# Gated expert rows turned by VectorE, and only filled result rows written, by GpSimd

## The chip, the cores and the metric

The kernel runs on one core of one Trainium2 chip. The metric is device time in microseconds (us). TensorE (PE) multiplies matrices into eight PSUM banks, VectorE (DVE) and ScalarE (ACT) read the banks, GpSimd (POOL) and SyncE (SP) mostly start DMA transfers.
## The reference

Two transformer blocks over 1024 tokens of width 1024. The first mixes tokens with gated linear attention and stick-breaking attention. The second has sliding-window attention, an mLSTM, cross attention and a mixture of 32 experts. Only that last part is touched:

```
expert_idx, gates = two experts for each token, with their weights
for each expert e, xb = the rows of its tokens:
    hb = silu(xb @ w_g[e]) * (xb @ w_u[e])      # 1024 -> 512 hidden columns
    yb = hb @ w_d[e]                            # 512 -> 1024
out[token] += yb[row] * gate                    # two rows for each token
```

1024 tokens with two experts each make 2048 assignments, 64 per expert on average. All matrices are float32.

## The kernel before, in words

Each expert has a block of `CAP` = 96 rows in three groups of `TG` = 32. An expert with more tokens gets spare blocks of 32 rows at the end; rows without a token are empty. For one block, TensorE (function `expert` of the tensor program) does this in order:

1. `group_products` (L1622): for each of three groups, 64 products of 32 rows of the turned block `XT` with the gate and up weights, spread over the four 32-partition quadrants (`QUADS`) of the group's bank.
2. `turn_hidden(0)` (L1628): when the hidden rows of groups 0 and 1 are there, two 128x128 products with the identity turn them into a bank; ACT's `hidden_home` copies them to `HIDT`.
3. `turn_block` (L1613): turns the gathered rows `XG` of the next block; VectorE (`block_ready`, L3148) scales them into `XT`.
4. `turn_hidden(1)` for group 2, and ACT's copy.
5. `down_products` (L1638): 96 products with the down weights into two banks. They wait for the hidden rows and for the result of the block before to be out of these banks (`y0_out`, `y1_out`).

ACT's `silu_of` turns a group's gate part into `SILU`; VectorE's `hidden_of` (L3154) multiplies it with the up part into `HID`. ACT copies the first result bank to `YO` (L1742, a helper's line that many operations have), VectorE the second (L3204). Both first wait for `y_stored`, the store of the block two before, which had the same `YO`. ACT then issues four stores (`store_block`, L2221), one for each quadrant, 32 partitions x 3 groups x 1 KB each: all 96 rows, empty or not, go to `y_of_slot` in DRAM.

GpSimd's loop (L3531): when block k is turned it copies the indices of block k+2 (L3535) and gathers its rows from `xn` with an indirect DMA of 96 descriptors of 4 KB (`gather_block`, L3519). A row without a token has an index beyond the bound and is skipped. SyncE loads each expert's three weight matrices (2 MB each, L3652) into one of two sets of buffers: gate and up when the group products of the expert two before are over, down when its down products are.

At the end GpSimd gathers two result rows for each token (L3555), which are added with their gates and normed. Much earlier (L3440) GpSimd fills the spare blocks of `y_of_slot` with zeros out of the buffer of `masks`, which ACT later overwrites with a gate tile.

## Time and profile before

| What | Value |
|---|---|
| median of three runs | 2068.24 us (2066.67 to 2074.23) |
| profiled execution, span | 2067.1 us |
| PE busy | 1994.4 us, 96% |
| DVE, ACT, POOL busy | 932.4, 583.1, 376.2 us |
| DMA moved | 360.51 MB |

The span of the profiled execution lies within the runs' spread; its median lies 1.1 us above, and no separate time of that execution is given beyond its span. The experts stand in the last quarter, 1463.84 to 2016.15 us: in the slices of 52 us the DMA engines are 90% busy or more there, while before they are mostly under 30%. "Idle before" is time in which an engine stood still ahead of an instruction, with what ended it. "To landing" is the time from the issue of a transfer to its completion.

### The profile page before, as it was taken

The numbers are of one execution on the slowest core, as the hardware profiler recorded it, in microseconds if no ns is written. First come the engines' busy times: TensorE is split into PE (matmuls) and PEld (weight loads), VectorE is DVE, ScalarE is ACT, GpSimd is POOL, SyncE is SP. The second block draws the span as 40 slices with busy tenths as digits, with TensorE's granted clock in tenths as the row PEclk, the third lists the DMA queues.
The fourth block names the chain that finished last, engine by engine and source line by source line (L and its number), as shares of the span: only waits on it lengthen the run. The fifth ranks groups of instructions, "written<-read, shape, count | busy, mean of one in ns | idle before, by whom it ended". The sixth has DMA issues, their size and how long they took to land.

```text
span 2067.1 us, 37980 instructions
## 1 busy us (share of the span) xinstructions
PE 1994.4 (96%) x15588; PEld 1136.0 (55%) x15588; DVE 932.4 (45%) x1543; ACT 583.1 (28%) x1076; POOL 376.2 (18%) x317
## 2 busy tenths in 40 slices
PE   8999999999899999999999999998999999999997
PEld 6476564765434445454446454565666666666563
DVE  3434553455676753586666674344511111111115
ACT  4123231433575220243123422242111111111113
POOL 0304333325252003004000233000100000000003
PEclk9999999999999999999999999999999999999999
DMA  9221220212525023600030412012899999999987
GB/s 396 84 82 36 81 95 28 94 31 87 173 102 173 31 103 64 166 1 1 0 122 11 143 42 64 1 41 91 346 398 402 406 407 414 416 405 412 404 355 269
DMA packets 104554, 360.51 MB, mean 174 GB/s; under 512 B 20536, under 2 KB 59856, under 8 KB 90128
## 3 DMA queue, kind: packets, MB, share of 16 engines
q1 hardware_dynamic: 58016, 280.37, 34.7%
q0 software_dynamic: 16368, 55.85, 8.0%
q10 hardware_dynamic: 30080, 23.09, 3.4%
q8 instruction: 58, 0.95, 0.2%
q14 instruction: 32, 0.26, 0.0%
HBM read 319.16 MB, written 45.49 MB: 176 GB/s over the span
## 4 chain that ended last, share of the span: by engine, by line
PE 72%; DMA 13%; DVE 8%; ACT 4%; issue 2%; ACTq 1%; POOL 0%; DVEq 0%; POOLq 0%; SPq 0%; PEldq 0%
PE bank L741 18%; DMA y_of_slot<-HT 13%; PE bank L734 12%; PE bank L951 9%; PE bank L1622 8%; PE bank L1638 4%; ACT work L1742 3%; PE bank L977 2%; PE bank L1037 2%; DVE O L2291 1%; DVE work L2291 1%; PE bank L809 1%; PE bank L1375 1%; PE bank L1152 1%; PE bank L849 1%
## 5 line engine op out<-in xcount | busy, mean ns | idle before, releaser
L1742 ACT ACTIVATE HT<-bank 64x256 f32<-64x256 f32 (+2 forms) x215 | 91.9, 432 | 452.5 <-PE bank L1622 197.0
L1742 ACT ACTIVATE work<-bank 128x512 f32<-128x512 f32 (+5 forms) x246 | 123.2, 520 | 327.4 <-PE bank L741 96.0
L1742 ACT ACTIVATE work<-work 128x1024 f32<-128x1024 f32 (+5 forms) x200 | 158.9, 806 | 170.4 <-DVEq L149 114.7
L734 PE MATMUL bank<-slots,HT 128*128 128x512 f32 (+2 forms) x576 | 184.1, 475 | 2.0 <-ACT HT L1742 1.5
L1622 PE MATMUL bank<-slots,HT 128*32 128x256 f32 x3136 | 172.4, 379 | 2.5 <-DVE HT L3148 1.6
L1622 PE MATMUL bank<-work,HT 128*32 128x256 f32 x3072 | 168.9, 379 | 0.4 <-issue 0.4
L3268 POOL TENSOR_TENSOR work<-work 128x1024 f32<-128x1024 f32 (+1 forms) x64 | 112.0, 1750 | 241.8 <-DVEq L149 160.6
L3154 DVE TENSOR_TENSOR HT<-HT,bank 64x256 f32<-64x256 f32 x97 | 41.1, 423 | 242.8 <-ACT HT L1742 242.4
L1622 PEld LDWEIGHTS bank<-slots,HT 128*32 128x32 f32 x3136 | 103.1, 110 | 68.8 <-issue 3.2
L734 PEld LDWEIGHTS bank<-slots,HT 128*128 128x128 f32 x576 | 98.3, 190 | 76.6 <-issue 71.2
L1622 PEld LDWEIGHTS bank<-work,HT 128*32 128x32 f32 x3072 | 102.4, 110 | 64.2 <-issue 1.0
L741 PE MATMUL bank<-HT,slots 128*128 128x512 f32 x256 | 116.4, 606 | 3.7 <-ACTq L149 2.5
L951 PE MATMUL bank<-slots,HT 128*128 128x512 f32 x256 | 114.8, 595 | 0.6 <-issue 0.6
L3204 DVE COPY HT<-bank 128x256 f32<-128x256 f32 x32 | 13.6, 425 | 204.9 <-DMA y_of_slot<-HT 139.0
L3535 POOL COPY index<-token_list 128x1 uint32 x32 | 5.9, 184 | 465.9 <-PE bank L1613 465.9
L1638 PE MATMUL bank<-slots,HT 128*32 128x256 f32 x1568 | 88.1, 380 | 0.7 <-ACT HT L1742 0.6
L1638 PE MATMUL bank<-work,HT 128*32 128x256 f32 x1536 | 86.2, 380 | 0.0
L951 PE MATMUL bank<-HT,slots 128*128 128x512 f32 x192 | 85.7, 594 | 0.5 <-ACT gate_row L1742 0.5
L741 PEld LDWEIGHTS bank<-HT,slots 128*128 128x128 f32 x256 | 49.2, 194 | 64.3 <-issue 62.9
L2447 DVE COPY_PREDICATED work<-masks,bank 128x512 f32<-128x512 uint32 x56 | 49.9, 891 | 71.4 <-PE bank L977 71.1
L1742 ACT ACTIVATE work<-O 128x1024 f32<-128x1024 f32 (+1 forms) x51 | 50.5, 990 | 95.7 <-DVEq L149 87.4
L951 PEld LDWEIGHTS bank<-slots,HT 128*128 128x128 f32 x256 | 46.6, 190 | 50.1 <-issue 50.0
(352 smaller groups left out, 3091.1 us busy)
## 6 DMA issues: line engine op xcount, KB each, us to landing
slots<-in_w_e_gate_dram SPq DMA_DIRECT2D x17, 2048.0 KB, 13.5
slots<-in_w_e_up_dram SPq DMA_DIRECT2D x17, 2048.0 KB
slots<-in_w_e_down_dram SPq DMA_DIRECT2D x17, 2048.0 KB, 17.4
work<-in_w_e_gate_dram SPq DMA_DIRECT2D x16, 2048.0 KB, 13.2
work<-in_w_e_up_dram SPq DMA_DIRECT2D x16, 2048.0 KB
work<-in_w_e_down_dram SPq DMA_DIRECT2D x16, 2048.0 KB
slots<-in_w_in_dram SPq DMA_DIRECT2D x8, 2048.0 KB, 8.7
slots<-in_w_ada_dram SPq DMA_DIRECT2D x6, 2048.0 KB, 15.3
```

The lines of the kernel that those rows point to most:

```text
L734: ins = pe.matmul(bank, lhsT, rhs, start=(n == 0), stop=(n == len(pairs) - 1))
L741: ins = pe.matmul(bank, of, x[:, k, :], start=(first and k == 0), stop=(last and k == 3), skip_group_check=True)
L951: ins = pe.matmul(bank, *pairs, start=(k == 0), stop=(k == NK - 1))
L977: ins = pe.matmul(bank[:, (j - j0) * P:(j - j0 + 1) * P], k[:, j * P:(j + 1) * P], q[:, j * P:(j + 1) * P], start=True, stop=True)
L1037: ins = pe.matmul(bank[:, 0:256], x[:, k], w[:, k], start=(first and k == 0), stop=(last and k == 3), skip_group_check=True)
L1622: ins = pe.matmul(GROUP_BANKS[g][QUADS[q], 0:QW], XT[:, k, g * TG:(g + 1) * TG], w[:, k, (q % 2) * QW:(q % 2 + 1) * QW], start=(k == 0), s ...
L1638: ins = pe.matmul(DOWN_BANKS[g // 2][QUADS[q], (g % 2) * QW:(g % 2 + 1) * QW], HIDT[:, g // 2, f % 2, at:at + TG], wd[:, f, q * QW:(q + 1) ...
L1742: return act.activation(o, i, f, bias=bias, scale=scale, **more)
L2291: line(dve.tensor_tensor(o, a, b, op))
L2447: empty(lambda b: dve.copy_predicated(s, bcast(m.unsqueeze(1), [P, NT, P // n, n // 2]), b.rearrange("p (j a h) -> p j a h", j=NT, h=n // 2)))
L3154: dve.tensor_tensor(HID[at:at + 64, g // 2, :], SILU[64:P, g, :], GROUP_BANKS[g][64:P, 0:QW], ALU.mult)\
L3268: line(pool.tensor_tensor(o, a, b, op))
```

## The change: what it does

Two things change in the experts' part.

First, TensorE no longer turns the hidden rows. VectorE writes a group's hidden rows to partitions 64 to 127 of `HID`, waits for its own write, and turns them with two 32x32-block transposes of 64x128 elements into `HIDT`. Such a transpose turns each block in place of its own, so the hidden features come out in another order, and the rows of the down weights are permuted on the host in the same order (`turned_hidden_rows`). ACT's two copies go too.

Second, the result is written by GpSimd with three indirect DMAs per block, one for each group: 128 partitions x 1 KB, each piece with its own destination index out of `piece_list`, which VectorE makes once. The index of a piece whose row is empty is beyond the bound, and the piece is skipped. In GpSimd's loop these writes stand behind the wait for `y0_out` and `y1_out` of the block, and the gather of the next turn of the loop behind them. The zero fill now covers all of `y_of_slot`: 154 blocks of 32 rows instead of 58.

```diff
 
 
+def turned_hidden_rows():
+
+    f, c, h, j = np.meshgrid(*(np.arange(n) for n in (DE // P, 2, 2, TG)), indexing="ij")
+    return (DE // 2 * h + P * c + TG * f + j).reshape(-1)
...
+    put("slot_of_piece", r % TG + TG * np.arange(TGS)[None, :])
+    put("piece_of_y", (r % TG + TG * np.arange(EXPERTS * TGS)[None, :]) * (D // QW) + r // TG)
...
-        HID = cut(HT_flat[:, 6 * D:6 * D + 2 * QW], 2)
-        HIDT = HT_flat[:, 7 * D:7 * D + 4 * P].rearrange("p (a c n) -> p a c n", a=2, c=2)
-        GROUP_BANKS, TURN_BANKS, HIDDEN_BANKS = banks[0:TGS], banks[4:6], (banks[3], banks[0])
+        HID = cut(HT_flat[:, 6 * D:6 * D + TGS * QW], TGS)
+        HIDT = cut(HT_flat[:, 7 * D:7 * D + TGS * P], TGS)
+        GROUP_BANKS, TURN_BANKS = banks[0:TGS], banks[4:6]
...
-        y_experts = y_dram[0:EXPERTS * CAP].rearrange("(b p) d -> b p d", p=CAP)
+        y_pieces = y_dram.rearrange("r (q c) -> (r q) c", c=QW)
...
-            def turn_hidden(a, turned):
-                for c in range(2):
-                    ins = pe.transpose(HIDDEN_BANKS[a][:, c * P:(c + 1) * P], HID[:, a, c * P:(c + 1) * P],
-                                       const("ident"))
-                ins.then_inc(turned, 1)
-
             def down_products(wd, groups, full):
 
                 for g in groups:
                     for f in range(DE // P):
-                        at = 64 * (g % 2) + TG * (f // 2)
                         for q in range(4):
                             ins = pe.matmul(DOWN_BANKS[g // 2][QUADS[q], (g % 2) * QW:(g % 2 + 1) * QW],
-                                            HIDT[:, g // 2, f % 2, at:at + TG], wd[:, f, q * QW:(q + 1) * QW],
+                                            HIDT[:, g, f * TG:(f + 1) * TG], wd[:, f, q * QW:(q + 1) * QW],
                                             start=(f == 0), stop=(f == DE // P - 1))
...
                     list_products()
-                pe.wait_ge(hidden_ready, it * 6 + 3 * x + 2)
-                turn_hidden(0, hidden_turned)
                 pe.wait_ge(rows_gathered[1 - x], it * 16 + 16 * (x + 1))
                 turn_block(1 - x, tokens_turned)
-                pe.wait_ge(hidden_ready, it * 6 + 3 * x + 3)
-                turn_hidden(1, hidden_turned)
                 pe.wait_ge(weights_in[x][2], it * 16 + 16)
 
                 pe.wait_ge(y0_out, it * 2 + x + 1)
                 pe.wait_ge(y1_out, it * 2 + x + 1)
-                pe.wait_ge(hidden_back, it * 4 + 2 * x + 1)
+                pe.wait_ge(hidden_ready, it * 6 + 3 * x + 2)
                 down_products(wd, (0, 1), down_full)
-                pe.wait_ge(hidden_back, it * 4 + 2 * x + 2)
+                pe.wait_ge(hidden_ready, it * 6 + 3 * x + 3)
                 down_products(wd, (2,), down_full)
 
             for x in range(2):
...
-            def hidden_home(a, back):
-                func(HIDT[:, a, :, :], cut(HIDDEN_BANKS[a], 4)[:, 0:2, :], ACT.Copy).then_inc(back, 1)
-
-            def store_block(block, y, sem):
-                rows = y_experts[bass.ds(block, 1)].rearrange("a (g r) (q c) -> q r (a g) c", r=TG, c=QW)
-                for q in range(4):
-                    act.dma_start(rows[q], cut(y[QUADS[q], :], TGS)).then_inc(sem, 16)
...
+            def expert(it, x, first=False):
+
+                for g in range(TGS):
+                    act.wait_ge(group_full, it * 6 + 3 * x + g + 1)
+                    silu_of(g, silu_ready)
+                if not first:
+                    act.wait_ge(y_stored[x], it * 48)
+                act.wait_ge(down_full, it * 4 + 2 * x + 1)
+                func(YO[x][:, 0:HALF], DOWN_BANKS[0], ACT.Copy).then_inc(y0_out, 1)
...
-                    for g in range(TGS):
-                        act.wait_ge(group_full, it * 6 + 3 * x + g + 1)
-                        silu_of(g, silu_ready)
-                    for a in range(2):
-                        act.wait_ge(hidden_turned, it * 4 + 2 * x + a + 1)
-                        hidden_home(a, hidden_back)
-                    act.wait_ge(y_stored[x], it * 64 + 64)
-                    act.wait_ge(down_full, it * 4 + 2 * x + 1)
-                    func(YO[x][:, 0:HALF], DOWN_BANKS[0], ACT.Copy).then_inc(y0_out, 1)
-                    act.wait_ge(y0_out, it * 2 + x + 2)
-                    act.wait_ge(y1_out, it * 2 + x + 2)
-                    store_block(it * 2 + x, YO[x], y_stored[x])
-            act.wait_ge(y_stored[0], 64 * (EXPERTS // 2 + 1))
+                    expert(it, x)
+            act.wait_ge(y_stored[0], 24 * EXPERTS)
...
+            ts(ASSIGNED, SPN, (CAP + 1 - TG) / TG - BELOW, float(TG), ALU.add, ALU.mult)
...
-            def hidden_of(g, ready):
-                at = 64 * (g % 2)
-                dve.tensor_tensor(HID[at:at + 64, g // 2, :], SILU[64:P, g, :], GROUP_BANKS[g][64:P, 0:QW], ALU.mult)\
-                    .then_inc(ready, 1)
+            def hidden_of(g, made, count, ready):
+
+                dve.tensor_tensor(HID[64:P, g, :], SILU[64:P, g, :], GROUP_BANKS[g][64:P, 0:QW], ALU.mult).then_inc(made, 1)
+                dve.wait_ge(made, count)
+                for c in range(2):
+                    ins = dve.transpose(HIDT[64 * c:64 * c + 64, g, :], HID[64:P, g, c * P:(c + 1) * P])
+                ins.then_inc(ready, 1)
...
-                for x in range(2):
-                    dve.sem_inc(y_stored[x], 64)
...
+                each = [P, EXPERTS, TGS]
+                tt(cut(PIECES, EXPERTS), bcast(const("slot_of_piece").unsqueeze(1), each), bcast(ASSIGNED.unsqueeze(2), each),
+                   ALU.is_ge)
+                stt(piece_list[:, :], PIECES, BEYOND_Y, const("piece_of_y"), ALU.mult, ALU.add)
...
-                dve.wait_ge(y_stored[x], it * 64 + 64)
+                if not (first or second):
+                    dve.wait_ge(y_stored[x], it * 48)
...
-            line(dve.memset(HID[64:P, 1, :], 0.0))
...
-            pool.dma_start(y_spares.rearrange("b p d -> p b d"),
-                           zeros[0:TG, :].unsqueeze(1).to_broadcast([TG, SPARE, D])).then_inc(spare_cleared, 16)
+            pool.dma_start(y_dram.rearrange("(b p) d -> p b d", p=TG),
+                           zeros[0:TG, :].unsqueeze(1).to_broadcast([TG, SPARE + EXPERTS * TGS, D])).then_inc(spare_cleared, 16)
...
                     pool.wait_ge(index_ready, it * 2 + x + 1)
                     pool.sem_inc(pool_passed, 1)
                     gather_block(x, XG[x], rows_gathered[x])
+                    pool.wait_ge(y0_out, it * 2 + x + 2)
+                    pool.wait_ge(y1_out, it * 2 + x + 2)
+                    pool.tensor_copy(pieces[x][:, :], piece_list[:, bass.ds((it * 2 + x) * TGS, TGS)]).then_inc(pieces_ready, 1)
+                    pool.wait_ge(pieces_ready, it * 2 + x + 1)
+                    pool.sem_inc(pool_passed, 1)
+                    for g in range(TGS):
+                        pool.indirect_dma_start(y_pieces, bass.IndirectOffsetOnAxis(ap=pieces[x][:, g:g + 1], axis=0),
+                                                YO[x][:, g * QW:(g + 1) * QW], None, bounds_check=EXPERTS * CAP * 4 - 1,
+                                                oob_is_err=False).then_inc(y_stored[x], 16)
...
-    for name in ("w_e_gate_2", "w_e_up_2", "w_e_down_2"):
+    for name in ("w_e_gate_2", "w_e_up_2"):
         arrays[f"in_{name}_dram"] = by_partition(_np.asarray(inputs[name])[0])
+    arrays["in_w_e_down_2_dram"] = by_partition(_np.asarray(inputs["w_e_down_2"])[0][:, turned_hidden_rows(), :])
```

On TensorE, one expert inside the loop stood so before (L1622 group products, L1628 turns of hidden rows, L1613 turn of the next block, L1638 down products):

```order
L1622 MATMUL bank<-slots,HT 32x256 [waits tokens_ready]
L1622 MATMUL bank<-slots,HT 32x256 x95
L1628 MATMUL bank<-cst,HT 128x128 [waits hidden_ready]
L1628 MATMUL bank<-cst,HT 128x128
L1613 MATMUL bank<-cst,HT 128x96 [waits rows_gathered1]
L1613 MATMUL bank<-cst,HT 128x96 x7
L1628 MATMUL bank<-cst,HT 128x128 [waits hidden_ready]
L1628 MATMUL bank<-cst,HT 128x128
L1638 MATMUL bank<-slots,HT 32x256 [waits hidden_back]
L1638 MATMUL bank<-slots,HT 32x256 x31
```

and stands so now (L1635, L1626 and L1644 are the same three steps):

```order
L1635 MATMUL bank<-slots,HT 32x256 [waits tokens_ready]
L1635 MATMUL bank<-slots,HT 32x256 x95
L1626 MATMUL bank<-cst,HT 128x96 [waits rows_gathered1]
L1626 MATMUL bank<-cst,HT 128x96 x7
L1644 MATMUL bank<-slots,HT 32x256 [waits hidden_ready]
L1644 MATMUL bank<-slots,HT 32x256 x31
```

The four turns of hidden rows are gone, and the turn of the next block, which waits for its gathered rows, is all that stands between the two kinds of product.

GpSimd's loop, both of its blocks, before:

```order
L3535 ISA [waits tokens_turned]
L3535 COPY index<-token_list 128x1
L3519 DMA HT<-xn,index 96x1024 [waits index_ready]
L3535 ISA [waits tokens_turned]
L3535 COPY index<-token_list 128x1
L3519 DMA HT<-xn,index 96x1024 [waits index_ready]
```

and the first of them now, up to the next block's first wait:

```order
L3533 ISA [waits tokens_turned]
L3533 COPY index<-token_list 128x1
L3517 DMA HT<-xn,index 96x1024 [waits index_ready]
L3539 ISA [waits y1_out,y0_out]
L3539 COPY pieces<-piece_list 128x3
L3543 DMA y_of_slot<-HT,pieces 19712x256 [waits pieces_ready]
L3543 DMA y_of_slot<-HT,pieces 19712x256 x2
L3533 ISA [waits tokens_turned]
```

The second gather of the loop now comes behind a wait for the block's result and behind three writes in the same queue.

## Rows read from the trace of the kernel before

**Rows 1.** The page: span and busy times.

```profile
span 2067.1 us, 37980 instructions
PE 1994.4 (96%) x15588; PEld 1136.0 (55%) x15588; DVE 932.4 (45%) x1543; ACT 583.1 (28%) x1076; POOL 376.2 (18%) x317
```

**Rows 2.** Chain that ended last, in order (start us, us, what): two experts; a store.

```profile
1638.37 10.36 PE bank L1622 x192
...
1655.44 10.36 PE bank L1622 x192
1665.80 0.37 PE bank L1628 x2
1666.17 0.66 PE bank L1613 x8
1666.83 0.36 PE bank L1628 x2
...
1710.22 31.73 DMA y_of_slot<-HT
```

**Rows 3.** Instructions in order of time: before the experts, experts 0, 14 to 15, 28, the spare.

```profile
1447.13 1.22 PE L1597 MATMUL bank<-work,cst 128*128 128x256 f32 x2 [4.08 <-DVEq L149]
...
1463.84 10.57 PE L1622 MATMUL bank<-slots,HT 128*32 128x256 f32 x192 [1.58 <-DVE HT L3148]
...
1717.29 0.33 SPq L3652 DMA_DIRECT2D slots<-in_w_e_gate_dram  x1
...
1719.25 0.98 POOL L3519 DMA_INDIRECT HT<-xn,index  x1 [0.86 <-POOL index L3535]
1723.52 10.54 PE L1622 MATMUL bank<-work,HT 128*32 128x256 f32 x192
...
1958.24 0.44 PE L1628 MATMUL bank<-cst,HT 128*128 128x128 f32 x2 [1.87 <-DVE HT L3154]
...
2021.65 0.44 PE L1628 MATMUL bank<-cst,HT 128*128 128x128 f32 x2 [0.95 <-DVE HT L3154]
```

**Rows 4.** Waits, 1500 to 2067 us (us in total, times, longest us).

```profile
ACT HT L1742 <- DMA y_of_slot<-HT: 154.5, 20, 11.6
```

**Rows 5.** Stretches (length, PE PEld DVE ACT POOL busy, PEclk, DMA share, GB/s).

```profile
1600.00:1700.00 100.00, 100.00 (x1773) 60.55 (x1766) 14.86 (x33) 17.68 (x37) 6.59 (x11) 1.00 1.01 407
1448.00:1450.00 2.00, 2.00 (x6) 1.50 (x6) 1.59 (x5) 1.28 (x1) 0.00 (x0) 0.50 0.99 426
```

**Rows 6.** DMA queues, 1600 to 1700 us: packets, MB, share of 16 engines.

```profile
q1 hardware_dynamic: 2534, 36.95, 90.3%
q10 hardware_dynamic: 2533, 2.23, 6.6%
q0 software_dynamic: 672, 1.50, 4.5%
```

**Rows 7.** DMA issues (count, KB, us to landing): 1500 to 1600; 1900 to 2000.

```profile
slots<-in_w_e_gate_dram SPq DMA_DIRECT2D x3, 2048.0 KB, 15.2
...
work<-in_w_e_gate_dram SPq DMA_DIRECT2D x3, 2048.0 KB, 11.6
```

**Rows 8.** The tile xn, 1480 to 2067 us: its gathers.

```profile
DMA to landing us min/median/max: 2.7/10.4/14.8
```

**Rows 9.** Groups of instructions by form, VectorE, 1455 to 1520 us.

```profile
L3154 DVE TENSOR_TENSOR HT<-HT,bank 64x256 f32<-64x256 f32 x9 | 3.8, 423 | 20.4 <-ACT HT L1742 20.3
L2291 DVE TENSOR_TENSOR work<-work 128x32 f32<-128x32 f32 x2 | 0.4, 193 | 0.1
```

**Rows 10.** The zero fill: its issue, its landing, what stands behind it.

```profile
808.94 1.04 POOL L3440 DMA_DIRECT2D y_of_slot<-masks  x1 [0.30 <-POOL masks L3439]
...
DMA to landing us min/median/max: 41.0/41.0/41.0
...
953.83 1.28 POOL L3268 TENSOR_TENSOR work<-slots 128x512 f32<-128x512 f32 x1 [143.85 <-DVEq L2304]
...
1078.63 1.23 ACT L1742 ACTIVATE masks<-bank 128x512 f32<-128x512 f32 x2 [0.18 <-ACT work L1742]
```

More of the change, by code:

```diff
@@ L634, in program @@
         spare_map = ctx.enter_context(nc.sbuf_tensor("spare_map", [P, SPARE + 1], I32))
+        piece_list = ctx.enter_context(nc.sbuf_tensor("piece_list", [P, EXPERTS * TGS], U32))
+        pieces = [ctx.enter_context(nc.sbuf_tensor(f"pieces{x}", [P, TGS], U32)) for x in range(2)]
+        pieces_ready = sem("pieces_ready")
         index = [ctx.enter_context(nc.sbuf_tensor(f"index{x}", [P, 1], U32)) for x in range(3)]
@@ L662, in program @@
         y_stored = [sem(f"y_stored{x}") for x in range(2)]
-        (tokens_turned, tokens_ready, group_full, silu_ready, hidden_ready, hidden_turned, hidden_back, down_full,
+        (tokens_turned, tokens_ready, group_full, silu_ready, hidden_made, hidden_ready, down_full,
          y0_out, y1_out, index_ready) = (sem(n) for n in (
-             "tokens_turned", "tokens_ready", "group_full", "silu_ready", "hidden_ready", "hidden_turned", "hidden_back",
+             "tokens_turned", "tokens_ready", "group_full", "silu_ready", "hidden_made", "hidden_ready",
              "down_full", "y0_out", "y1_out", "index_ready"))
-        (sp_rows, sp_weights, sp_down_weights, sp_turned, sp_ready, sp_group, sp_silu, sp_hidden, sp_hidden_turned,
-         sp_hidden_back, sp_down, sp_y, sp_stored, sp_index, sp_passed) = (sem("spare_" + n) for n in (
-             "rows", "weights", "down_weights", "turned", "ready", "group_full", "silu", "hidden", "hidden_turned",
-             "hidden_back", "down", "y", "stored", "index", "passed"))
+        (sp_rows, sp_weights, sp_down_weights, sp_turned, sp_ready, sp_group, sp_silu, sp_hidden_made, sp_hidden,
+         sp_down, sp_y, sp_stored, sp_index, sp_passed) = (sem("spare_" + n) for n in (
+             "rows", "weights", "down_weights", "turned", "ready", "group_full", "silu", "hidden_made", "hidden",
+             "down", "y", "stored", "index", "passed"))
         pool_passed, spare_cleared = sem("pool_passed"), sem("spare_cleared")
@@ L2251, in _ @@
                     act.wait_ge(sp_stored, s * 64 + 64)
[L2252 removed]
+            act.wait_ge(y_stored[1], 24 * EXPERTS)
             act.sem_inc(moe_over, 1)
@@ L3053, in _ @@
             BELOW = 0.5 / TG - 0.5
+            BEYOND_Y = 2.0 ** 20
             line(dve.memset(OF_EXPERT, 1.0))
@@ L3185, in gates_and_slots, with expert @@
                 copy(slot_id[:, :], SLOT)
+                each = [P, EXPERTS, TGS]
+                tt(cut(PIECES, EXPERTS), bcast(const("slot_of_piece").unsqueeze(1), each), bcast(ASSIGNED.unsqueeze(2), each),
+                   ALU.is_ge)
+                stt(piece_list[:, :], PIECES, BEYOND_Y, const("piece_of_y"), ALU.mult, ALU.add)
                 dve.sem_inc(routed, 1)
-            def expert(it, x, first=False):
+            def expert(it, x, first=False, second=False):
                 for g in range(TGS):
@@ L3206, in _ @@
             line(dve.memset(token_list[:, :], 0))
-            line(dve.memset(HID[64:P, 1, :], 0.0))
             dve.wait_ge(tokens_turned, 1)
             block_ready(tokens_ready)
-            for x in range(2):
-                expert(0, x, first=(x == 0))
+            expert(0, 0, first=True)
+            expert(0, 1, second=True)
             with dve.Fori(1, EXPERTS // 2) as it:
```

19 lines of the change are left out of this document (9 added, 10 removed).

## The prediction

> **What bounds the kernel now.** I read the page first, then the chain, the waits, the stretches, the DMA queues and the landings. TensorE is busy 96% of a span of 2067.1 us [rows 1]. The experts run from 1463.84 to 2016 us, about 552 us [rows 3]. In the chain one expert is four steps of TensorE ahead of the down products, 10.36 + 0.37 + 0.66 + 0.36 us [rows 2]. The group products of one expert and the next start at 1638.37 and 1655.44 us [rows 2], so a period is 17.07 us, and the down products are the remaining 5.32. TensorE has no idle time from 1600 to 1700 us [rows 5]. So TensorE bounds this part, but in the same stretch the DMA share is 1.01 [rows 5]: the DMA engines never rest either. Two bounds lie side by side, and an edit on TensorE alone can be worth no more than the distance to the other.
>
> That distance needs two numbers. The first is the lead of the weights. Gate weights are issued at 1717.29 us [rows 3] and are needed two experts on, when the group products behind those of 1723.52 start: 1740.6, that is 23.3 us later. The gate matrix lands after 15.2 us early in the experts and 11.6 late [rows 7]; the up matrix follows it, 2.1 MB at 407 GB/s [rows 5] = 5.2 us. So both are there 2.9 us ahead of need early and 6.5 late. The lead grows by 3.6 us in some 23 experts, 0.16 us each: the DMA engines' pace is 17.07 - 0.16 = 16.9 us per expert.
>
> The second is how the queues share the engines. In 100 us q1 (weights) passed 2534 packets and q10 (stores) 2533 [rows 6], though one weight packet has 16 KB and one store packet 1 KB. Per expert that is 3 x 128 + 48 = 432 and 4 x 96 + 64 = 448 asked for. Equal counts mean that a queue with work gets one packet in turn, whatever its size. The stores therefore crawl: one takes 31.73 us [rows 2], ACT waits 154.5 us for them [rows 4], and at times this reaches TensorE (1.87 us at 1958.24 [rows 3]).
>
> **The change, part by part.** *TensorE's turns.* 0.37 + 0.36 = 0.73 us per expert, 32 experts: 23.4 us less work on the engine that bounds [rows 2]. All of it is on the path now.
>
> *VectorE's transposes.* Two of 64x128 per group. The trace shows none. From below, an operation of 32 columns takes 193 ns; from above, one of 256 columns 423 ns [rows 9]. I take 0.25 us, 0.5 for two; at worst 0.85. The hidden rows of group 2 are ready about 0.4 (ACT) + 0.42 + 0.1 + 0.5 = 1.4 us after the group products, at worst 1.8. TensorE asks for them after the turn (0.66) and two thirds of the down products (3.5), at 4.2 us. So 0 on the path; the cover is 2.4 us or more. Group 1 is ready sooner still. VectorE is 15% busy there [rows 5]. In the spare block nothing covers them: TensorE's turn took 0.44 us [rows 3], and ACT's copy behind it is as long, 0.9 to 1.0 with the handover, against 0.6: -0.4. The memset dropped (64x256) and the small operation added before the first expert: -0.1.
>
> *Fewer bytes.* 2048 of 3072 rows are filled, so of q10's 6.6% a third goes: 0.066 x 17.07 / 3 = 0.37 us per expert. The skipped pieces still pass as descriptors, as skipped rows of the gather do: q0 has 672 packets for six gathers, 112 each = 96 + 16, all rows counted, but only 1.50 MB [rows 6]. I give these 0.1 us. DMA pace: 16.9 - 0.37 + 0.1 = 16.6 us per expert, against TensorE's 16.34. So the DMA engines become the bound.
>
> *The queue.* q0 now gets 3 x (128 + 16) + 112 = 544 packets per expert, 34 per engine. The weights queue has 27 per engine. At one in turn, q0 keeps up only if the weights queue stands empty for part of each expert. A turn is 17.07 / 27 = 0.63 us, so writes and gather need 34 x 0.63 = 21.5 us, and 2 to 3 more for issue and completion (the fastest gather took 2.7 [rows 8]). In the loop GpSimd issues the gather of block k+3 behind the writes of block k, about 7 us after the down products of k; TensorE wants it at its turn in k+2, 16.34 + 10.4 = 26.7 us after them. It has 20 us where it now has 32 (it is issued at 1719.25, inside the down products [rows 3]). So TensorE stops at rows_gathered from the first experts on, in stops of one to four us, until the weights' lead is so long that q1 runs empty. What this costs is lead: DMA work is the same, but TensorE can't use up the lead of the weights.
>
> *The sum.* The weights of the last expert come 30 x (16.9 - 16.6) = 9 us sooner. If TensorE ends with the same lead over need as before (6.5 us), the experts end 9 + 0.7 (the last expert is shorter) = 9.7 us sooner. The lead at which q1 runs empty is longer: gate weights with nothing ahead need 2 + 2 x 5.2 = 12.4 us, a lead of 22.6 - 12.4 = 10 us. That takes back up to 3.7: 6.0 us. If the lead could be used up, 9.7 + 6.5 = 16.2. I take 7.5 us, between 9.7 and 6.0, and 0.5 for the edges: 8 us. The profiled span of 2067.1 becomes 2059; the median lies 1.1 higher: 2060 us.
>
> *Zero fill.* 154 blocks for 58: 41.0 x 154 / 58 = 109 us, ending near 918. Two loads of 2 MB go beside it; GpSimd reads them first at 953.83, 35 us behind the end of the whole fill; ACT writes over the zeros' source at 1078.63 [rows 10]. Moving 4.2 MB takes some 10 us at 407 GB/s. Cost 0, with 25 us of cover even if the loads waited for the whole fill; past that each us would count.
>
> *ACT.* Two copies and four issues per expert go; ACT is 18% busy there [rows 5], worth 0. GpSimd gains three indirect issues of 0.98 us [rows 3] per expert and is 7% busy [rows 5]: 0 by itself.
>
> **A rule that speaks against this.** The trace shows one packet per turn between q1 and q10 [rows 6]; for q0 it has only gathers of seven packets per engine, 10.4 us to land [rows 8], which is about seven turns and the fixed part. The Trainium skill, "DMA: Bandwidth & Descriptors", section "Queues, rings and completion order", says that a DMA engine drains a whole packet of some 9 to 17 descriptors from one ring before it goes to the next. By that rule q0 would not starve. What q0 would then give is the first rival; the rows on q1 and q10 do not agree with the rule.
>
> **Rivals.** *First: q0 keeps up, the weights are used just in time.* For it: GpSimd's queue has other descriptors than the two that were counted, and no row shows it backlogged. Against: the length of the gathers. Lead used up: 16.2 + 0.5, and some stops: 2068 - 16 = 2052 us.
>
> *Second: the full gain.* TensorE stays the bound: 23.4 us, and some 3 us of stops like that of 1.87 us [rows 3]: 2041 us. For it: the DMA share may count waiting, and the pace be elastic. Against: the landings moved only 0.16 us per expert while TensorE took 17.07.
>
> *Third, slower: q0's turns cost what they do now, and the stops cost clock.* If a turn stays 0.63 us and the seven more that q0 needs add 0.06 us each, an expert takes 27 x 0.63 + 0.4 = 17.4 us, 0.35 more than now: +11 us. Besides, after TensorE stood idle for 4.08 us before 1447.13 us [rows 3] its granted clock was 0.50 from 1448 to 1450 [rows 5], the lower of its two levels (1.2 GHz for 2.4). Three spells of some 3 us at half pace are +5. Less the half us of edges: 2084 us with the clock, 2079 without. It decides from a turn of 0.62 us on, which is 0.01 below today's; against it stand the third fewer real pieces.
>
> *Fourth: the pieces are not skipped or the fill delays the mLSTM part:* no gain, 2068 or a little over.
>
> **Chances.** Forecast 0.54, first rival 0.21, full gain 0.05, third 0.13, fourth 0.07. A run of this kernel tells about 0.5%, 10 us, from no change. The forecast's own range is 2050 to 2069; a third of its chance is beyond 10 us faster (0.18), the rest within (0.35). First rival: 0.18 faster, 0.03 within. Full gain 0.05 faster. Third: 0.09 slower, 0.04 within. Fourth: 0.05 within, 0.02 slower. Rounded: faster 0.41, within 0.5% 0.48, slower 0.11. The range, 2046 to 2077, leaves the full gain and the worst of the third outside.
>
> **What would show it.** L1628 and ACT's copies gone, transposes of 0.2 to 0.3 us; q0 at about 544 packets per expert and q10 at none; TensorE idle ahead of the turn of the next block (L1626 now) behind the transfer of xn, 1 to 4 us in about every third expert; gathers landing in 15 to 25 us; gate weights in 7 to 11 us, not 12 to 15; a mean period of 16.8 us. The forecast is wrong if TensorE waits for weights (first rival), if it never waits (second), or if PEclk falls under 1 between 1480 and 2000 us (third).

## The result: slower by 0.9%, by stops of TensorE beside GpSimd's issues

The changed kernel took 2087.91 us in its first measurement (median of 4, 2086.47 to 2089.8) against 2067.45 for the kernel before (2065.7 to 2074.23): ratio 1.0091 [1.0076, 1.0106], some 19 us slower. The forecast was 2060, with 2077 as its upper end. The page of the profiled execution:

```profile
span 2086.7 us, 37598 instructions
PE 2009.3 (96%) x15458; PEld 1168.4 (56%) x15458; DVE 991.8 (48%) x1739; ACT 539.4 (26%) x996; POOL 478.1 (23%) x445
```

TensorE has 130 instructions fewer than in [rows 1] and is busy 15 us longer. The chain that ended last shows where, in the columns of [rows 2]:

```profile
1709.43 0.81 PE bank L1626 x8
1710.24 5.32 PE bank L1644 x96
1715.56 5.28 PE bank L1635 x92
1720.84 0.10 issue
1720.94 0.68 PE bank L1635 x6
1721.62 0.09 issue
1721.70 5.42 PE bank L1635 x94
1727.13 0.81 PE bank L1626 x8
1727.94 5.32 PE bank L1644 x96
1733.26 5.23 PE bank L1635 x93
```

The turns are gone: one step of 0.81 us stands for 0.37 + 0.66 + 0.36, and the down products still take 5.32. But the group products (L1635) go from 1715.56 to 1727.13, 11.57 us for 10.36 in [rows 2], and are broken in the middle. The period is 1733.26 - 1715.56 = 17.70 us, not 17.07. So 0.58 us are won and 1.2 lost, 0.6 us per expert. Over the whole part it is less, because TensorE stands still in a few experts of the kernel before too (periods of 17.9, 17.6 and 19.0 us), and its mean period is 17.18 us: by the two traces the experts take 15.4 us longer (1465.66 to 2033.35 against 1463.84 to 2016.09 us), they begin 1.8 us later, and what stands behind them, the spare block first, takes 2.3 us more, 19.6 us in all. The same expert by engine, in order of time, with the idle time before each in brackets (these views count a step from the start of its first product, the chain from the end of the product before it, so the group products are 10.54 us here where the chain has 10.36, and 11.75 where it has 11.57):

```profile
1715.16 4.66 PEld L1635 LDWEIGHTS bank<-slots,HT 128*32 128x32 f32 x87
1716.29 0.18 POOL L3539 COPY pieces<-piece_list 128x3 uint32 x1 [10.91 <-DVE HT L3203]
1717.35 1.02 POOL L3543 DMA_INDIRECT y_of_slot<-HT,pieces  x1 [0.88 <-POOL pieces L3539]
1718.67 0.99 POOL L3543 DMA_INDIRECT y_of_slot<-HT,pieces  x1 [0.30 <-issue]
1719.97 0.98 POOL L3543 DMA_INDIRECT y_of_slot<-HT,pieces  x1 [0.30 <-issue]
1720.19 0.16 PEld L1635 LDWEIGHTS bank<-slots,HT 128*32 128x32 f32 x6 [0.37 <-issue]
1720.95 0.19 PEld L1635 LDWEIGHTS bank<-slots,HT 128*32 128x32 f32 x6 [0.59 <-issue]
1720.98 0.38 ACT L1742 ACTIVATE HT<-bank 64x256 f32<-64x256 f32 x1 [6.48 <-remote]
1721.72 1.47 PEld L1635 LDWEIGHTS bank<-slots,HT 128*32 128x32 f32 x30 [0.59 <-issue]
```

GpSimd issues the three writes from 1717.35 to 1720.95. TensorE's weight loads run on for 2.47 us, stop at 1719.82, and go on in spurts of six with 0.37, 0.59 and 0.59 us between them. Nothing that the program waits for ended these gaps ("issue"): no wait stands within the group products. ACT's silu of group 0 starts 5.6 us after the start of the group products (1715.38), where it is 3.7 us in the kernel before when ACT has no store to wait for:

```profile
1655.26 10.54 PE L1622 MATMUL bank<-work,HT 128*32 128x256 f32 x192
1658.96 0.38 ACT L1742 ACTIVATE HT<-bank 64x256 f32<-64x256 f32 x1 [3.83 <-PE bank L1622]
```

The stops are in every expert from the second on, the first that has a GpSimd write beside it; the first expert, with none beside it, took 10.57 us.

The DMA engines are not what stops it. The queues in 1600 to 1700 us (as [rows 6]), that stretch (as [rows 5]), and the landings of the gathers (as [rows 8]):

```profile
q1 hardware_dynamic: 2512, 36.47, 90.9%
q0 software_dynamic: 1485, 3.11, 9.5%
...
1600.00:1700.00 100.00, 98.97 (x1690) 64.33 (x1686) 26.36 (x69) 9.94 (x23) 22.38 (x32) 1.00 1.00 396
...
DMA to landing us min/median/max: 2.1/7.1/12.8
```

PEclk is 1.00, the gathers come sooner than before, and from 1500 us to the end of the experts TensorE waits neither for weights nor for xn.

### The profile page after: what moved, and what is told of

It reads as the page before. It is cut to its first block, busy times and chain, and to the rows that moved or that the text cites. A ratio compares the mean times of both kernels' runs of the same rounds, so it can differ in the third digit from the quotient of the medians.

```text
span 2086.7 us, 37598 instructions
## 1 busy us (share of the span) xinstructions
PE 2009.3 (96%) x15458; PEld 1168.4 (56%) x15458; DVE 991.8 (48%) x1739; ACT 539.4 (26%) x996; POOL 478.1 (23%) x445
## 4 chain that ended last, share of the span: by engine, by line
PE 85%; DVE 7%; ACT 3%; issue 2%; DMA 1%; POOL 0%; DVEq 0%; ACTq 0%; POOLq 0%; SPq 0%; PEldq 0%
PE bank L754 18%; PE bank L1635 17%; PE bank L747 12%; PE bank L964 9%; PE bank L1644 8%; PE bank L1050 2%; PE bank L990 2%; ACT work L1742 2%; PE bank L1165 1%; DVE work L2282 1%; DVE O L2282 1%; PE bank L1626 1%; PE bank L822 1%; PE bank L1388 1%; DMA slots<-in_w_ada_dram 1%
## 5 line engine op out<-in xcount | busy, mean ns | idle before, releaser
L1742 ACT ACTIVATE HT<-bank 64x256 f32<-64x256 f32 (+1 forms) x150 | 67.8, 452 | 558.5 <-PE bank L1635 213.2
L1635 PE MATMUL bank<-slots,HT 128*32 128x256 f32 x3136 | 187.6, 380 | 5.3 <-DVE HT L3141 1.4
L1635 PE MATMUL bank<-work,HT 128*32 128x256 f32 x3072 | 184.4, 380 | 3.1
L1635 PEld LDWEIGHTS bank<-slots,HT 128*32 128x32 f32 x3136 | 125.2, 110 | 64.7 <-issue 26.2
L1635 PEld LDWEIGHTS bank<-work,HT 128*32 128x32 f32 x3072 | 124.5, 110 | 60.0 <-issue 23.5
L3543 POOL DMA_INDIRECT y_of_slot<-HT,pieces x96 | 95.7, 996 | 48.1 <-POOL pieces L3539 26.4
L1644 PE MATMUL bank<-slots,HT 128*32 128x256 f32 x1568 | 89.4, 384 | 3.4 <-DVE HT L3150 2.7
L1644 PE MATMUL bank<-work,HT 128*32 128x256 f32 x1536 | 86.2, 380 | 0.0
L3539 POOL COPY pieces<-piece_list 128x3 uint32 x32 | 5.8, 182 | 338.6 <-DVE HT L3203 338.6
## 6 DMA issues: line engine op xcount, KB each, us to landing
y_of_slot<-masks POOLq DMA_DIRECT2D x1, 19712.0 KB, 105.7
```

The lines of the kernel that those rows point to most:

```text
L1635: ins = pe.matmul(GROUP_BANKS[g][QUADS[q], 0:QW], XT[:, k, g * TG:(g + 1) * TG], w[:, k, (q % 2) * QW:(q % 2 + 1) * QW], start=(k == 0), s ...
L1644: ins = pe.matmul(DOWN_BANKS[g // 2][QUADS[q], (g % 2) * QW:(g % 2 + 1) * QW], HIDT[:, g, f * TG:(f + 1) * TG], wd[:, f, q * QW:(q + 1) * QW],
L1742: return act.activation(o, i, f, bias=bias, scale=scale, **more)
L3543: pool.indirect_dma_start(y_pieces, bass.IndirectOffsetOnAxis(ap=pieces[x][:, g:g + 1], axis=0), YO[x][:, g * QW:(g + 1) * QW], None, boun ...
```

## The experiments

Three theories at first: A, GpSimd's issues hold TensorE up; B, the traffic of the pieces does; C, VectorE's transposes do. Each group below ran on one chip with the kernel before beside it. The code shown is shortened. A "job" is a set of runs taken together on one chip. A period is the mean from the turn of block 3 to that of block 31: 17.18 us in the kernel before, 17.66 in the changed one.

### Which part of the change: four runs in one job

**Turns alone.** After's `hidden_of` and down weights, before's `store_block` and zero fill:

```diff
-                    for g in range(TGS):
-                        pool.indirect_dma_start(y_pieces, ...).then_inc(y_stored[x], 16)
+                    store_block(it * 2 + x, YO[x], y_stored[x])     # ACT
```

> VectorE turns the hidden rows (with the permuted down weights), but ACT stores the blocks as before and only the spare blocks are filled with zeros. Theory A (GpSimd's three indirect writes per expert hold up TensorE and its signals while they are issued): no such writes, so the group products take 10.36 us again, ACT's silu of group 0 starts 3.5 us after their start, and the 0.73 us per expert of TensorE's turns are gained as far as the weights allow: 2045 to 2060 us. Theory B (the traffic of the written and skipped pieces disturbs the DMA engines or TensorE): the same. Theory C (VectorE's transposes disturb TensorE or the signals): the stalls in the group products stay, 11.6 us for them, 2080 us or more.

**Writes alone.** Before with after's piece list, zero fill and GpSimd writes; TensorE turns the hidden rows:

```diff
-                    store_block(it * 2 + x, YO[x], y_stored[x])     # ACT
+                    for g in range(TGS):
+                        pool.indirect_dma_start(y_pieces, ...).then_inc(y_stored[x], 16)
```

> TensorE turns the hidden rows as in the kernel before, and only the stores are changed: GpSimd writes the pieces with three indirect transfers per expert, and all of the result is filled with zeros. Theories A and B: the group products take 11.6 to 11.7 us instead of 10.36 in all experts but the first, with silu of group 0 some 2.1 us late, so the whole is the kernel before plus 31 x 1.25 = 39 us: 2100 to 2110 us, slower than the changed kernel by the turns' 0.73 us x 32. Theory C: no stalls, 2060 to 2070 us.

**All pieces skipped.**

```diff
+                ts(PIECES, PIECES, 0.0, None, ALU.mult)
+                ts(PIECES, PIECES, 1.0, None, ALU.add)
                 stt(piece_list[:, :], PIECES, BEYOND_Y, const("piece_of_y"), ALU.mult, ALU.add)
```

> The changed kernel with every piece's index beyond the bound: the same three indirect transfers per expert, but no piece is written (the experts' results don't reach memory, only the spare blocks' do). Theory A (the issue itself): the stalls stay as they are, group products 11.6 us, 2086 to 2089 us. Theory B (the pieces' traffic): the stalls shrink or go, 2045 to 2065 us. Theory C: stalls stay.

**Two writes later.**

```diff
                     for g in range(TGS):
+                        if g == 1 and not last:
+                            pool.wait_ge(group_full, it * 6 + 3 * x + 4)
                         pool.indirect_dma_start(...)
```

> The changed kernel, but GpSimd issues only the first write at once and the other two when the first group of the next block is over, that is between two signals of TensorE's (the first issue ends 3.0 us after the start of the group products, the signal is due at 3.5, the other two run from some 4 to 6.5, and the next signal is due at 6.9). Theory A in its narrow form (an issue that falls on a signal of TensorE's holds it, and TensorE stops some 25 products later): no signal is late and no stall, 2045 to 2055 us. Theory A in its wide form (three issues in a row, or two, stop TensorE wherever they fall): stalls move with the writes to the second group, 2070 to 2088 us. Theory B: as the changed kernel, 2088. Theory C: stalls stay in the first group, 2088.

| Run | us | ratio to before | period | group products |
|---|---|---|---|---|
| turns alone | 2066.67 | 0.9987 [0.9976, 0.9998] | 17.12 | 10.5 |
| writes alone | 2100.98 | 1.0158 [1.0139, 1.0178] | 18.09 | 11.6 |
| all skipped | 2084.7 | 1.0085 [1.0064, 1.0105] | 17.54 | 11.6 |
| two writes later | 2066.91 | 0.9992 [0.9982, 1.0002] | 16.98 | 10.6 to 11.1 |

The second and third came near their ranges (2100.98 in 2100 to 2110, 2084.7 just under 2086). C falls: transposes without writes have no stops, writes without transposes have them. B falls as far as the written bytes go: with nothing written the stops are the same, though q0 passed 1.59 MB in 1600 to 1700 us for 3.11. It does not fall for the packets: skipped pieces pass as packets too (1444 for 1485), so these runs do not tell GpSimd's issuing from the packets that it puts on the queue. A stands with that limit. In "writes alone" the loads stop at 1723.45, again 2.47 us behind the first issue at 1720.98:

```profile
1718.79 4.66 PEld L1629 LDWEIGHTS bank<-slots,HT 128*32 128x32 f32 x87
1720.98 1.02 POOL L3557 DMA_INDIRECT y_of_slot<-HT,pieces  x1 [0.88 <-POOL pieces L3553]
1723.72 0.17 PEld L1629 LDWEIGHTS bank<-slots,HT 128*32 128x32 f32 x6 [0.27 <-issue]
```

With two issues in a row a single gap is left. Here it begins 2.48 us behind the first of the two and ends at 2.77:

```profile
1706.43 7.22 PEld L1635 LDWEIGHTS bank<-slots,HT 128*32 128x32 f32 x134
1711.17 0.99 POOL L3545 DMA_INDIRECT y_of_slot<-HT,pieces  x1 [1.55 <-PE bank L1635]
1712.47 0.98 POOL L3545 DMA_INDIRECT y_of_slot<-HT,pieces  x1 [0.30 <-issue]
1713.94 3.16 PEld L1635 LDWEIGHTS bank<-slots,HT 128*32 128x32 f32 x58 [0.28 <-issue]
```

This run missed both of its ranges: no signal was late (silu at 3.7 us), so the narrow form of A is out, and the stops moved with the writes as the wide form says, but two in a row cost 0.1 to 0.5 us and not enough for its 2070 us. In expert 1 GpSimd came so late that its three issues stood in a row after all, and the group products took 11.62 us.

"Turns alone" missed from the other side: no stops, and yet 2 us won where 8 to 23 were expected. Its undisturbed period is 16.49 us = 10.36 + 0.81 + 5.32. But ACT and VectorE wait for the stores, worse than before, 251 us for ACT where [rows 4] has 154.5 in a little more time; the next block's silu and hidden rows stand behind those waits, and TensorE behind them:

```profile
ACT HT L1742 <- DMA y_of_slot<-HT: 251.4, 24, 13.6
...
1819.56 8.12 PE L1644 MATMUL bank<-slots,HT 128*32 128x256 f32 x96 [3.19 <-DVE HT L3151]
...
1830.63 0.60 ACT L1742 ACTIVATE HT<-bank 128x512 f32<-128x512 f32 x1 [12.69 <-DMA y_of_slot<-HT]
```

The idle time costs more than itself here: behind the 3.19 us the granted clock was 0.50 from 1819.5 to 1825 us, the lower of its two levels, and the down products took 8.12 us for 5.39. So most of TensorE's 0.58 us per expert is given back: the stores set the pace, with a DMA share of 1.01 in 1600 to 1700 us.

### One at a time, and what kind of issue: a second job

```diff
 # one by one
-                        if g == 1 and not last:
-                            pool.wait_ge(group_full, it * 6 + 3 * x + 4)
+                        if g and not last:
+                            pool.wait_ge(group_full, it * 6 + 3 * x + 3 + g)
 # behind the turn: writes of block k-1 between the wait for turn k and gather k+2
+                pool.wait_ge(tokens_turned, it * 2 + x + 1)
+                write_pieces(it * 2 + x - 1, 1 - x)
 # plain
+                    for q in range(4):
+                        pool.dma_start(rows[q], cut(YO[x][QUADS[q], :], TGS)).then_inc(y_stored[x], 16)
 # quarter
-  IndirectOffsetOnAxis(ap=pieces[x][:, g:g + 1], axis=0), YO[x][:, ...]
+  IndirectOffsetOnAxis(ap=pieces[x][0:TG, g:g + 1], axis=0), YO[x][0:TG, ...]
```

> The changed kernel with one write in each group of the next block: write 0 at once, write 1 when group 0 is over, write 2 when group 1 is over, then the turn and the gather. In the run with the last two in a row TensorE stopped some 2.5 us after the first issue of the pair (0.28 us), in the changed kernel 2.47 us after the first of three. Theory A1 (TensorE runs on for some 2.5 us while GpSimd makes descriptors and stops when they go on for longer): one issue of 1.0 us never stops it, group products 10.36 us, period 16.49 us wherever the weights are there; what remains is set by the DMA engines: 2050 to 2062 us. Theory A2 (each issue takes some 0.4 us from TensorE, in a row or not): as the changed kernel or the run with two in a row, 2067 to 2088 us.

> The changed kernel with the three writes of a block in a row, but issued behind the turn in the next block, so that they lie beside its down products (about 1 to 4.7 us behind their start), and the gather behind them. Theory A1: the down products stop as the group products did, 6.6 us instead of 5.32, and ACT's copy of the first result bank is late by about 1 to 2 us: as the changed kernel, 2084 to 2092 us. Rival (only the group products, or only a signal that ACT or VectorE waits for, are hit): down products 5.32 to 5.5, 2050 to 2065 us.

> VectorE's turns, and GpSimd stores whole blocks with four plain transfers (the ones that ACT issued before), at the place of the three indirect ones. If any transfer that GpSimd issues holds TensorE up while its descriptors are made: four in a row stop it as long or longer than three, the group products take 11.6 to 12.2 us, 2088 to 2110 us. If it is only the indirect kind: group products 10.36, and the time is that of the run with ACT's stores, 2060 to 2068 us.

> The changed kernel with three indirect writes of 32 pieces instead of 128 (partitions 32 to 127 of the result are not written). If the hold follows the descriptors: the issues get shorter than 1.0 us or the stall in the group products goes from 1.25 to at most 0.3 us, 2045 to 2062 us. If it follows the instruction whatever it writes: as the changed kernel, 2083 to 2089 us.

| Run | us | ratio | period |
|---|---|---|---|
| one by one | 2061.78 | 0.9970 [0.9958, 0.9982] | 16.93 |
| behind the turn | 2063.48 | 0.9981 [0.9971, 0.9991] | 16.97 |
| plain, whole blocks | 2068.1 | 0.9995 [0.9986, 1.0004] | 17.24 |
| quarter | 2053.61 | 0.9930 [0.9915, 0.9945] | 16.54 |

No run of this job has a stop, and "behind the turn" shows that this proves little: the times that theory A gave for the other three (2050 to 2062 us for "one by one") came true without testing it. The wait I chose was for a turn already done, so its writes came out where after has them, 1.97 us into the group products and three in a row, and not beside the down products as I meant. Yet TensorE went on:

```profile
1707.14 10.57 PE L1635 MATMUL bank<-slots,HT 128*32 128x256 f32 x192
...
1709.11 1.02 POOL L3537 DMA_INDIRECT y_of_slot<-HT,pieces  x1 [0.90 <-POOL pieces L3533]
1710.43 0.99 POOL L3537 DMA_INDIRECT y_of_slot<-HT,pieces  x1 [0.30 <-issue]
1710.86 0.38 ACT L1742 ACTIVATE HT<-bank 64x256 f32<-64x256 f32 x1 [4.68 <-PE bank L1635]
1711.73 0.98 POOL L3537 DMA_INDIRECT y_of_slot<-HT,pieces  x1 [0.30 <-issue]
```

Either the order of the waits or the job made the difference. The next runs ask that.

### The program or the job

The third job ran the changed kernel and "behind the turn" again, the changed kernel with eight dead semaphore additions ahead of GpSimd's loop, and "one by one" with all pieces skipped.

```diff
+            for _ in range(8):
+                pool.sem_inc(pool_passed, 1)
             with pool.Fori(0, EXPERTS // 2) as it:
```

> The changed kernel once more, on the same chip as the three others of this group. The run with the writes behind the wait for the turn had the same three issues at the same place of the expert (first issue 1.97 us after the start of the group products, 0.30 us between them), but no stall. If that came from another chip or run, this one can be without stalls too: about 2063 us. If the stalls belong to the program: 2086 to 2090 us, group products 11.6 us.

> The run with the writes of a block behind the wait for the next turn once more, beside the changed kernel. If the order of GpSimd's waits and the loop's boundary decide: 2061 to 2066 us, group products 10.57 with three issues in a row beside them. If the difference was the chip: the same time as the changed kernel beside it.

> The changed kernel with eight additions to a semaphore that nobody waits for, put ahead of GpSimd's loop: nothing in the experts differs but where GpSimd's instructions lie. If the stall comes from the issues themselves: 2086 to 2090 us. If it depends on how instructions lie or are fetched: stalls of another size or none, down to 2063 us.

> One write in each group of the next block, as in the run one by one, and every piece's index beyond the bound, so the experts' results don't reach memory. There the experts' period was 16.49 us where nothing stopped it and 16.9 in the mean, with TensorE waiting for up-weights. If the bytes of the written pieces make these waits (2.1 MB per eight experts less to move): period 16.49 to 16.6 us, 2050 to 2055 us. If the weights alone set the pace: 2060 to 2063 us.

The eight additions tell nothing, since the changed kernel beside them had no stops either. The fourth and fifth repeated kernels unchanged:

> The changed kernel a third time, in another job than the two before. First time 2087.9 us with TensorE stopping 1.25 us in each expert's group products beside GpSimd's three issues, second time 2062.9 us with no stop. If the stop belongs to the chip or to the conditions of a job: either about 2088 or about 2063 us, all runs of the job alike. If it is drawn anew in each execution: a mixture within the job.

> GpSimd's writes alone, TensorE's turns kept, a second time. Measured first in a job in which the stops were seen: 2101.0 us, period 18.1. If this job shows stops in the changed kernel, again 2099 to 2104 us; if it shows none, the period is 17.07 us and the time 2064 to 2069 us, that of the kernel before.

> The changed kernel a fourth time, as the measure of whether this job's chip shows the stops: 2087 to 2090 us with them, about 2063 without.

> GpSimd's writes behind the wait for the next turn, three issues in a row at the same place of the expert. It ran without stops on two chips, on one of which the changed kernel beside it had none either. If stops belong to the chip: as the changed kernel beside it. If its order of waits avoids them: 2061 to 2066 us even where the changed kernel takes 2088.

> One write in each group of the next block. With single issues TensorE is not held for longer than 1.0 us at a time, so on a chip that shows the stops the group products should take 10.36 to 10.6 us and the whole 2060 to 2064 us, some 25 us less than the changed kernel beside it; without stops, the same as that kernel.

| Job | Kernel | us | ratio | period |
|---|---|---|---|---|
| third | changed | 2062.92 | 0.9964 [0.9952, 0.9977] | 16.98 |
| third | behind the turn | 2062.71 | 0.9966 [0.9953, 0.9978] | 17.01 |
| third | changed, shifted | 2063.7 | 0.9974 [0.9963, 0.9985] | 16.97 |
| third | one by one, all skipped | 2051.4 | 0.9903 [0.9886, 0.9920] | 16.49 |
| fourth | changed | 2089.35 | 1.0097 [1.0080, 1.0113] | 17.66 |
| fourth | writes alone | 2105.99 | 1.0177 [1.0160, 1.0194] | 18.21 |
| fifth | changed | 2089.15 | 1.0091 [1.0072, 1.0110] | 17.66 |
| fifth | behind the turn | 2091.15 | 1.0098 [1.0077, 1.0118] | 17.70 |
| fifth | one by one | 2064.19 | 0.9975 [0.9966, 0.9985] | 16.87 |

The same program takes 2063 us in one job and 2088 to 2089 in three others, the first measurement among them, each time in all its executions, while the kernel before stays at 2068 to 2070. So the stops need two things: three (or two) issues in a row, and a chip or job in which such issues hold TensorE. "Behind the turn" had no stops on a chip with the number 2 and had them later on a chip with the same number, so the number doesn't settle which of the two it is. Changed kernel, fifth job, then third job, waits in the experts (us, times, longest; in the third the loads' "issue" gaps stand where the products wait for weights):

```profile
ACT HT L1742 <- remote: 179.6, 28, 6.5
...
PEld bank L1635 <- issue: 44.0, 91, 0.6
```

```profile
PEld bank L1635 <- issue: 21.5, 25, 2.1
...
PE bank L1635 <- DMA work<-in_w_e_up_dram: 6.0, 9, 1.6
```

In a job with the stops, "one by one" doesn't have them (after's own place, 1.97 us in, for the first write):

```profile
1655.40 10.54 PE L1635 MATMUL bank<-work,HT 128*32 128x256 f32 x192
1657.38 1.02 POOL L3545 DMA_INDIRECT y_of_slot<-HT,pieces  x1 [0.88 <-POOL pieces L3538]
1659.11 0.38 ACT L1742 ACTIVATE HT<-bank 64x256 f32<-64x256 f32 x1 [4.58 <-PE bank L1635]
1659.95 0.99 POOL L3545 DMA_INDIRECT y_of_slot<-HT,pieces  x1 [1.55 <-PE bank L1635]
```

It is 25 us faster than the changed kernel beside it, and faster than the kernel before in both jobs: the version to keep.

The same program holds a test of its own. Its last block has no next block to wait for, so its three writes are in a row, beside the spare block's group products. Second job, then fifth job:

```profile
2007.61 3.66 PE L1635 MATMUL bank<-slots,HT 128*32 128x256 f32 x64 [0.99 <-DVE HT L3203]
...
2011.38 4.20 PE L1635 MATMUL bank<-slots,HT 128*32 128x256 f32 x64 [0.96 <-DVE HT L3203]
2014.92 0.17 PEld L1635 LDWEIGHTS bank<-slots,HT 128*32 128x32 f32 x5 [0.39 <-issue]
```

So in the second job even a row of three indirect writes stopped nothing. In the fifth, within one execution, single issues left 10.54 to 10.57 us, two in a row in expert 1 made it 10.92, and three in a row lengthened the spare block's 3.66 to 4.20. ("One by one" and "writes alone" each ended up to 2 us above what was expected of them there.)

### Four arms in one run

The last run held its own control:

```diff
+                if j == 0: indexed(b, x, P)      # three indirect, 128 pieces
+                elif j == 1: plain(b, x)         # three plain
+                elif j == 2: indexed(b, x, TG)   # three indirect, 32 pieces
+                # j == 3: 128 pieces, issued behind the next block's turn
```

> The changed kernel with GpSimd's stores in four arms, block by block in turn, so that one run holds its own control: blocks 4i three indirect writes of 128 pieces in a row, as in the changed kernel; blocks 4i+1 three plain transfers in a row (three of the four quadrants, 96 x 1 KB each); blocks 4i+2 three indirect writes of 32 pieces in a row; blocks 4i+3 three indirect writes of 128 pieces, but issued beside the down products of the next block, behind its turn. What the plain and the short arms leave out isn't written. On a chip with the stops the group products beside the first arm take 11.6 us. If any transfer that GpSimd issues holds TensorE, the plain arm does too (11.2 us or more); if only indirect ones, 10.36 to 10.6. If the number of descriptors counts, the short arm takes 10.36 to 10.6 us; if the time of the burst counts (3.3 us in all against 3.6), 11.2 or more. If the place doesn't matter, the down products beside the last arm take 6.0 to 6.6 us instead of 5.32. On a chip without the stops all arms have 10.36 and 5.32 us, and these questions stay open.

It took 2060.42 us (one execution), and no arm had a stop: the group products took 10.54 to 10.57 us beside every arm, the control included. So what in the issues holds TensorE (indirect or any, descriptors or length) stays open, as does whether down products are held: "plain" and "quarter" too ran only in the second job, where the control of three in a row had no stop either.

## Why the prediction was wrong, by its own steps

*"GpSimd gains three indirect issues ... and is 7% busy: 0 by itself."* This step failed, and with it the forecast. Cost of an issue was put down as GpSimd's time, and GpSimd has time. In three of the four jobs that ran the changed kernel a row of three held TensorE for 1.2 us per expert. That came out as 0.8 us in the period (17.66 against 16.87), because without the stops TensorE waits for weights instead, and as 25 us in all (2089.15 against 2064.19 with the issues apart). [Rows 3] could not show it: the trace of before has one issue at a time beside the experts. None of the rivals had it; the third, slower, put its price on DMA turns and clock. In the experts of the changed kernel neither moved (PEclk 1.00); only behind the spare block's stop did the clock fall, to 0.58 in 2041.2 to 2044.5 us, where 32 down products took 3.23 us for 1.93.

The rest can be read where there are no stops, the third job: 2062.92 against 2070.11, ratio 0.9964, 7.4 us faster, where the sum said 8.

*TensorE's turns, 23.4 us.* Mis-sized: the turn of the next block, now alone, takes 0.81 us for 0.66, so the period where nothing stops it is 16.49 us and not 16.34, and 0.58 us x 32 = 18.6 us are saved. Not on the path for the most part, as forecast: the DMA engines are the second bound. With no piece written (one by one, all skipped) the period is 16.49 throughout and the time 2051.4 us, 11 us less than the changed kernel beside it, which those bytes hide.

*The queue.* Wrong in its count. Gathers were to land in 15 to 25 us and stop TensorE; in the third job they landed in 11.2 (median) and stopped it once, at the spare block (1.6 us), never within the experts:

```profile
DMA to landing us min/median/max: 3.2/11.2/13.3
...
q1 hardware_dynamic: 2536, 36.87, 91.9%
q0 software_dynamic: 1486, 3.15, 9.0%
```

The turns themselves held: while q0 had work, it passed one packet to one of q1 (221 to 227 from 1662 to 1672 us in the third job), and in the kernel before q0, q1 and q10 passed 40 each from 1672 to 1674. The term at fault is "544 packets per expert". 1486 packets in 100 us are 252 per 16.98 us. [Rows 6] gave 112 for a gather of 96 descriptors of 4 KB; that leaves 140 for three writes, 47 each, not 144. What fits is that the 16 engines share a write's pieces, with up to four pieces of 1 KB to a packet, and have one packet more each: 128 pieces are 8 per engine, so 2 + 1 packets, 48 in all. In the quarter run 32 pieces are 2 per engine, 1 + 1 packets, 32 in all: 3 x 32 + 112 = 208, measured 1248 in 100 us, 206 per 16.54. So q0 asks for 16 turns per engine where the weights have 27, and keeps up. The Trainium skill, "DMA: Bandwidth & Descriptors", section "SWDGE vs HWDGE vs iDMA", says that a packet holds at most 64 descriptors and preferably no more than 4096 bytes; the counts agree, and by that rule the first rival's premise could have been had in advance.

*The lead.* What TensorE waits for is the up weights, the first rival's sign. In the third job, 1600 to 1900 us, gate and up matrices landed after

```profile
DMA to landing us min/median/max: 15.4/16.3/16.9
...
DMA to landing us min/median/max: 21.0/21.9/23.2
```

(gate 13.2 in the median of before in the same stretch). The slowest, at 23.2 us, are as late as the 23.3 us that the prediction gave for the need, and TensorE waited up to 1.6 us for them. So the lead that the forecast kept (6.5 us at the end) was all used up.

*Fewer bytes, -0.37 + 0.1, DMA pace 16.6.* Mis-sized: the period at the bound is 16.9 to 17.0 us (one by one 16.93 and 16.87, changed 16.98), no better than the 16.9 that was read as the pace of before. Whole blocks by GpSimd's plain transfers have 17.24, so leaving out the empty rows is worth 0.27 us on GpSimd's queue; against whole blocks by ACT (17.12) it is 0.14. The too fast pace and the lead left unused cancelled, so where there are no stops the 8 us were right by luck, by two wrong terms.

*Transposes, 0.25 us each.* 0.63 a pair, 0.32 each, nothing on the path:

```profile
1721.84 0.63 DVE L3150 STREAM_TRANSPOSE HT<-HT 64x128 f32<-64x128 f32 x2
```

*Zero fill 0.* It landed after 105.7 us, 109 forecast, and nothing clear speaks against the 0: block 1 was turned at 1475.91 to 1481.33 us in the runs with the whole fill, at 1478.60 in the one with transposes and the small fill, at 1477.34 before.

## What to carry to other kernels

Several indirect transfers issued in a row can have a price for the neighbours as well as for GpSimd: keep them apart, a wait on the progress of the engine that bounds is enough, and read that engine's gaps put down to "issue" against GpSimd's issues. Where two bounds lie side by side, work out how much of an edit the second one lets through before relieving the first; the turns were worth 0.58 us per expert and the DMA engines let through a third of that. Repeat a surprising time on another chip before explaining it.

## What the runs showed of the hardware

TensorE can be held beside a row of GpSimd's indirect issues although neither waits for the other: from about 2.5 us after the first of three issues on, some 1.2 us in all, and ACT's silu starts 1.9 us late meanwhile (5.6 us for 3.7). The Trainium skill, "SBUF — State Buffer", section "SBUF: two separate sides", says that within the engine side TensorE, ScalarE and VectorE's own port pair never wait for anyone; the hold measured here is not explained by that page, and whether it arises in SBUF, in the making of descriptors, in the packets, in the fetch of instructions or in the semaphores wasn't told apart. It was there in four jobs (the first measurement and the first, fourth and fifth job) and absent in the third, where the same program ran, and in the second and sixth, which ran other kernels with the same three issues in a row. In the third to the fifth all executions of the changed kernel in a job agreed, with no effect on the kernel before.
